# Which partition takes which token of an expert's block, in a one-core decoder step with a mixture of experts

## The chip, the cores and the metric

One core of a Trainium2 chip runs the whole program. The metric is the device time of one execution in microseconds (us), here 1616.77 us as the median of three runs. The core has a matrix engine (TensorE, PE), a vector engine (VectorE, DVE), a scalar engine (ScalarE, ACT), GpSimd (POOL) and SyncE (SP), and sixteen DMA engines that move data between device memory and the on-chip memory with its 128 partitions.

## What is computed

One layer of a hybrid decoder on 1024 prompt tokens and 32 sample tokens (1056 rows of 1024 float32 values): three token mixers, an output projection, and then a mixture of experts with 32 experts, of which each token uses two. The second half is where the change lies:

```python
def hier_moe(h, w_rg, b_rg, w_re, b_re, w1, w3, w2):
    ...
    g_sel = jnp.argmax(g_logits, axis=-1).astype(jnp.int32)
    e_in = e_logits[tok, g_sel]
    top_v, top_i = lax.top_k(e_in, TOP_K)
    ...
    def expert_block(args):
        xb, e = args
        return (jax.nn.silu(xb @ w1[e]) * (xb @ w3[e])) @ w2[e]
    ...
    return jnp.zeros((t, d), y_rows.dtype).at[tok_sorted].add(contrib)
```

An expert's weights are three matrices of 512 x 1024 float32, 6 MiB. The final normalisation of every row follows. Which rows of a block hold which of an expert's tokens makes no difference to the sum.

## The kernel before

The first 900 us or so are the dense part (mixers, projections), in items that PE takes one after the other. The routing then gives each (token, expert) pair a rank: the token's place among the tokens of its expert. `rank_ones` (L1262 to L1269) compares the ranks with the constant row `io128` and so makes a matrix of ones and zeros, token by slot; PE multiplies it with the tokens' numbers, and out comes `tok0`, a table of 128 partitions by 32 experts: partition p holds the token whose rank equals `io128[p]`. The same ones place each token's gate weight (`wslot`). Partitions whose number exceeds the ranks in use get an index out of bounds, and the indirect DMAs move nothing for them. With `io128` the row 0, 1, 2, ..., an expert with n tokens fills the partitions 0 to n-1.

The experts then run as 33 blocks b: one for each expert with up to 128 of its tokens, and the last one for the tokens beyond 128 of one expert. A block has 1056 x 2 / 33 = 64 tokens in the mean. For a block:

- SP loads six weight chunks `wr` of 1 MiB (L659), four for the up products, two for down. There are 13 slots; a load waits until PE has used the slot's last chunk. The slots that lie in the dense part's buffers get their first chunks as its last items free them (`moe_sync`).
- ACT rounds a chunk to `whr` (L1093), and DVE makes the remainder `wl` (L1281).
- POOL gathers the tokens' rows into `xg` (L786), one 4 KiB row for each filled partition; PE transposes them (step `T`, L893), and ACT and DVE split them into `xTh` and `xTl`.
- PE makes the up products (L902 to L904), DVE the gated hidden rows `gs`, PE transposes these (L910), DVE makes `gTl`, PE makes the down products `Y` (L919 to L921), and DVE multiplies by the gates: `ysb` (L1281).
- POOL adds `ysb` onto the rows of `x_rows` in device memory with an accumulating scatter (L790), again 4 KiB for each filled partition. `g2p` (L805) fetches gate rows where a slot changes kind.

PE's order is written out: in the turn of block b it does up(b,0), G(b-1), up(b,1), T(b+1), Y(b-1), up(b,2), up(b,3). The two last blocks are not scattered. Once block 30's scatter has landed, POOL fetches their rows of `x_rows` (L820), SP loads the tiles `yt`, ACT squares them and DVE scales and ends them (L1442), and POOL writes the late rows (L828).

The last block's table comes from a table in device memory whose rows go by rank itself, so that `io128` doesn't touch it.

Of the kernel before, what the change touches and what calls it, by code (L numbers as in the profile page):

```python
# [24 lines left out]
P = 128  # L25
# [56 lines left out]
def build(nc, x_prompt, x_sample, c_prompt, c_sample, state_conv_a, state_conv_c, norm1_g, norm2_g,  # L82
# [5 lines left out]
    with ctx:  # L88
        def sem(name):
            return ctx.enter_context(nc.semaphore(name))  # L90
# [12 lines left out]
        base = (nc.sbuf_base + 31) // 32 * 32  # L103
# [7 lines left out]
        def sb(name, shape, dt=F32):  # L111
            t, top[0] = at(name, shape, dt, top[0])
            return t
# [21 lines left out]
        io128 = sb("io128", [P, P])  # L135
# [426 lines left out]

        XT = [(g, t, rows) for g in range(2) for t, rows in tiles(g)]
        XN = {(g, t): n for n, (g, t, _) in enumerate(XT)}
        conv_flat = conv[:, :, :].rearrange("p c t -> p (c t)")

# [18 lines left out]
        rt_const, tab_out = sem("rt_const"), sem("tab_out")  # L585
# [1068 lines left out]
        def _(pool):  # L1654
            def x_load(g, t):
                s, rows = x_slot(g, t), dict(tiles(g))[t]
                if g and t == 0:
# [7 lines left out]
                               pattern=[[-1, P]], channel_multiplier=1).then_inc(id_ok, 1)  # L1665
# [27 lines left out]
            for p in range(KD // 2 - 1):  # L1693
                pool.wait_ge(modt_ok, p // 2 + 1)
                for k in (2 * p, 2 * p + 1):
# [9 lines left out]
                               pattern=[[0, HEADS], [-1, P]], channel_multiplier=1).then_inc(wsr_ok, 1)  # L1705
# [40 lines left out]
            for m, n in ((tri, P), (trif, NE)):  # L1746
                pool.affine_select(out=m[:], in_=m[:], compare_op=ALU.is_gt, fill=0.0, base=0,
                                   pattern=[[1, n]], channel_multiplier=-1).then_inc(rt_const, 1)
                pool.drain()
            pool.iota(io32[:], pattern=[[1, NE]], base=0, channel_multiplier=0,  # L1750
                      allow_small_or_imprecise_dtypes=True).then_inc(rt_const, 1)
            pool.drain()
            pool.iota(io16[:], pattern=[[1, MAXX]], base=0, channel_multiplier=0,
                      allow_small_or_imprecise_dtypes=True).then_inc(rt_const, 1)
            pool.drain()
            pool.iota(thr[:], pattern=[[P, NBLK - 1]], base=P, channel_multiplier=0,
                      allow_small_or_imprecise_dtypes=True).then_inc(rt_const, 1)
            pool.drain()
            pool.iota(bval[:], pattern=[[NE, NBLK - 1]], base=NE, channel_multiplier=1,
                      allow_small_or_imprecise_dtypes=True).then_inc(rt_const, 1)  # L1760
            pool.drain()
            pool.iota(io128[:], pattern=[[1, P]], base=0, channel_multiplier=0,
                      allow_small_or_imprecise_dtypes=True).then_inc(rt_const, 1)
            pool.drain()
            pool.iota(vhi[:], pattern=[[-(TPAD // P), 2], [-1, NT]], base=OOB // P, channel_multiplier=0,
                      allow_small_or_imprecise_dtypes=True).then_inc(rt_const, 1)
            pool.drain()
            pool.iota(vlo[:], pattern=[[0, 1]], base=OOB % P, channel_multiplier=-1,
                      allow_small_or_imprecise_dtypes=True).then_inc(rt_const, 1)
# [1508 lines left out]
```

## Time and profile before

| | us |
|---|---|
| median of three runs | 1616.77 (1615.28 to 1617.14) |
| the profiled execution | 1616.57 |
| its span, first to last instruction | 1614.8 |
| PE busy | 1555.9 |
| DVE busy | 1256.8 |
| ACT busy | 804.1 |
| POOL busy | 353.0 |

The profiled execution lies 0.20 us under the median. The page gives busy times by engine, the span in 40 slices of 40.4 us with the mean busy share of the sixteen DMA engines, the chain of work that ended last and the costliest groups. The blocks of the experts fill the slices from 25 on. A busy share is summed over packets, by the time each took; it isn't kept apart by DMA engine.

### The profile page before, as it was taken

What the parts mean: (1) busy time and instruction counts of PE and PEld (TensorE: products, weight loads), DVE (VectorE), ACT (ScalarE), POOL (GpSimd) and SP (SyncE); (2) the same over time, 40 slices, a digit from 0 to 9 for tenths busy, and PEclk for the clock granted to TensorE, in tenths of its full rate; (3) what the DMA queues carried; (4) which work ended last, traced back from release to release, by engine and by line L of the source; (5) the groups of instructions that cost most, each with busy time, mean ns of one, the idle gap of its engine ahead of it and who ended that gap; (6) DMA issues with size and microseconds to landing.
All of it is one profiled execution on the core that took longest, in us unless ns stands there. A gap on an engine that the chain in (4) does not pass through costs nothing.

```text
span 1614.8 us, 23286 instructions
## 1 busy us (share of the span) xinstructions
PE 1555.9 (96%) x9097; PEld 1333.5 (83%) x9097; DVE 1256.8 (78%) x1698; ACT 804.1 (50%) x878; POOL 353.0 (22%) x271
## 2 busy tenths in 40 slices
PE   5999999999999999999999998999999999999993
PEld 3777788878889999999999976888888888887771
DVE  4668877755838898887555568999999999899985
ACT  4222232334333323313243356887887787777773
POOL 2310000000000000002000202366655544333231
PEclk9999999999999999999999999999999999999997
DMA  9965223425434332224222866999999999999966
GB/s 339 321 198 181 80 86 90 139 79 147 130 91 144 118 88 77 78 88 140 78 79 84 275 225 241 359 391 387 384 368 376 380 387 379 382 371 368 372 242 236
DMA packets 219025, 362.48 MB, mean 224 GB/s; under 512 B 19807, under 2 KB 168383, under 8 KB 193562
## 3 DMA queue, kind: packets, MB, share of 16 engines
q1 hardware_dynamic: 196476, 323.10, 56.6%
q0 software_dynamic: 21792, 35.72, 7.6%
q10 hardware_dynamic: 646, 2.15, 0.3%
q8 instruction: 73, 1.20, 0.3%
q14 instruction: 38, 0.31, 0.1%
HBM read 363.16 MB, written 32.34 MB: 245 GB/s over the span
## 4 chain that ended last, share of the span: by engine, by line
PE 79%; DMA 10%; DVE 7%; issue 1%; DVEq 1%; ACT 1%; SPq 1%; POOLq 0%; POOL 0%; ACTq 0%
PE z L2930 16%; PE z L2932 16%; PE z L2931 16%; DMA wr<-in_w_dram 7%; PE z L904 5%; PE z L902 5%; PE z L903 5%; PE z L919 3%; PE z L921 3%; PE z L920 3%; DVE wl L1281 2%; PE q L2821 2%; DMA ada<-in_w_ada_dram 1%; PE q L893 1%; DVE conv L2350 1%
## 5 line engine op out<-in xcount | busy, mean ns | idle before, releaser
L1281 DVE TENSOR_TENSOR wl<-wr,whr 128x2048 fp32r<-128x2048 f32 x196 | 442.3, 2283 | 1.1 <-ACT whr L1093 0.8
L1093 ACT ACTIVATE whr<-wr 128x2048 fp32r<-128x2048 f32 x196 | 373.3, 1915 | 86.8 <-DMA wr<-in_w_dram 55.3
L2930 PE MATMUL z<-h_hi,w_hi 128*128 128x272 f32 (+1 forms) x1248 | 406.7, 326 | 2.3 <-DVE h_lo L2169 1.8
L2932 PE MATMUL z<-h_hi,w_lo 128*128 128x272 f32 (+1 forms) x1248 | 402.5, 323 | 0.0
L2931 PE MATMUL z<-h_lo,w_hi 128*128 128x272 f32 (+1 forms) x1248 | 401.3, 322 | 0.0
L2169 DVE TENSOR_TENSOR w_lo<-w_raw,w_hi 128x1024 fp32r<-128x1024 f32 (+1 forms) x168 | 179.4, 1068 | 127.3 <-ACT w_hi L1868 127.3
L2930 PEld LDWEIGHTS z<-h_hi,w_hi 128*128 128x128 f32 x1248 | 234.7, 188 | 28.2 <-issue 7.3
L2932 PEld LDWEIGHTS z<-h_hi,w_lo 128*128 128x128 f32 x1248 | 234.4, 188 | 16.6
L2931 PEld LDWEIGHTS z<-h_lo,w_hi 128*128 128x128 f32 x1248 | 234.8, 188 | 15.7 <-issue 0.2
L902 PE MATMUL z<-whr,xTh 128*128 128x512 f32 x528 | 208.8, 395 | 0.0
L904 PE MATMUL z<-wl,xTh 128*128 128x512 f32 x528 | 206.1, 390 | 0.0
L903 PE MATMUL z<-whr,xTl 128*128 128x512 f32 x528 | 205.5, 389 | 0.0
L2350 DVE SCALAR_TENSOR_TENSOR conv<-a_in,parT,conv 128x512 f32<-128x512 f32 x360 | 193.7, 582 | 14.5 <-issue 1.3
L1868 ACT ACTIVATE w_hi<-w_raw 128x1024 fp32r<-128x1024 f32 (+1 forms) x168 | 150.4, 929 | 45.6 <-DMA w_raw<-in_w_in_dram 45.3
L2046 ACT ACTIVATE sig<-z 128x512 f32<-128x512 f32 (+1 forms) x48 | 29.3, 610 | 266.1 <-PE z L2932 266.1
L805 POOL DMA_INDIRECT g2p<-mod_rows,g2i x33 | 78.6, 2383 | 257.5 <-ACT gfac L1081 239.8
L904 PEld LDWEIGHTS z<-wl,xTh 128*128 128x128 f32 x528 | 99.1, 188 | 21.1
L902 PEld LDWEIGHTS z<-whr,xTh 128*128 128x128 f32 x528 | 99.6, 189 | 19.5
L903 PEld LDWEIGHTS z<-whr,xTl 128*128 128x128 f32 x528 | 99.3, 188 | 19.6
L919 PE MATMUL z<-whr,gTh 128*128 128x512 f32 x256 | 102.8, 402 | 6.4 <-DVE gTl L1281 6.4
L921 PE MATMUL z<-wl,gTh 128*128 128x512 f32 x256 | 100.0, 391 | 0.0
L920 PE MATMUL z<-whr,gTl 128*128 128x512 f32 x256 | 99.9, 390 | 0.0
(480 smaller groups left out, 2291.5 us busy)
## 6 DMA issues: line engine op xcount, KB each, us to landing
wr<-in_w_dram SPq DMA_DIRECT2D x198, 1024.0 KB, 19.6
w_raw<-in_w_in_dram SPq DMA_DIRECT2D x104, 512.0 KB, 3.8
ada<-in_w_ada_dram SPq DMA_DIRECT2D x6, 2048.0 KB, 14.1
w_raw<-in_w_branch_dram SPq DMA_DIRECT2D x48, 256.0 KB, 2.8
w_raw<-in_w_out_dram SPq DMA_DIRECT2D x16, 512.0 KB, 3.9
ada_h<-in_w_ada_dram SPq DMA_DIRECT2D x2, 2048.0 KB, 15.3
ada_u<-in_w_ada_dram SPq DMA_DIRECT2D x2, 2048.0 KB, 9.9
ada_m<-in_w_ada_dram SPq DMA_DIRECT2D x2, 2048.0 KB, 10.7
```

What stands on the lines that cost most here:

```text
L902: pe.matmul(out, xTh[s][:, k, :], hi[:, i * FF:(i + 1) * FF], start=(k == 0), stop=False)
L903: pe.matmul(out, xTl[s][:, k, :], hi[:, i * FF:(i + 1) * FF], start=False, stop=False)
L904: last = pe.matmul(out, xTh[s][:, k, :], lo[:, i * FF:(i + 1) * FF], start=False, stop=(k == KD - 1))
L919: pe.matmul(out, gTh[:, k, :], hi[:, w0:w0 + 512], start=(k == 0), stop=False)
L1093: act.activation(whr[n % HN][:], wr[n % RN][:], ACT.Copy).then_inc(m_hi, 1)
L1281: return dve.tensor_tensor(out, a, b, op)
L1868: act.activation(w_hi[n % WS][:, 0:kn, :], w_raw[n % WS][:, 0:kn, :], ACT.Copy).then_inc(whi_ok, 1)
L2169: return dve.tensor_tensor(out, a, b, op)
L2350: last = dve.scalar_tensor_tensor(out, x, wt, out, ALU.mult, ALU.add)
L2930: pe.matmul(out, w_hi[w][:, k, :], hi[:, k, t0:t1], start=(k == 0), stop=False)
L2931: pe.matmul(out, w_hi[w][:, k, :], lo[:, k, t0:t1], start=False, stop=False)
L2932: last = pe.matmul(out, w_lo[w][:, k, :], hi[:, k, t0:t1], start=False, stop=(k == kn - 1))
```

## The change

One constant is made differently. The 128 values of the row `io128` are the same numbers in another order. Column 32j + 4a + b (j and b from 0 to 3, a from 0 to 7) holds 8(j//2) + 64(j%2) + a + 16b. Read the other way: an expert's tokens of rank 0 to 7 go to partitions 0, 4, 8, ..., 28, those of rank 8 to 15 to 64, 68, ..., 92, rank 16 to 23 to 1, 5, ..., 29, rank 24 to 31 to 65, 69, ..., 93, and so on; from rank 64 on the partitions 32 to 63 and 96 to 127 are filled in the same manner.

```diff
-            pool.iota(io128[:], pattern=[[1, P]], base=0, channel_multiplier=0,
-                      allow_small_or_imprecise_dtypes=True).then_inc(rt_const, 1)
+            for j in range(4):
+                i128 = pool.iota(io128[:, 32 * j:32 * j + 32], pattern=[[1, 8], [16, 4]], base=8 * (j // 2) + 64 * (j % 2),
+                                 channel_multiplier=0, allow_small_or_imprecise_dtypes=True)
+            i128.then_inc(rt_const, 1)
```

No other line differs. The loading of chunk slots as the last dense items free them stands in both kernels alike.

POOL's instructions around it, early in the program, in the kernel before; `io_58` is `io128`:

```order
L1756 IOTA thr 32x8
L1759 IOTA bval 32x8
L1762 IOTA io_58 128x128
L1765 IOTA vhi 128x18
L1768 IOTA vlo 128x1
L1771 IOTA vali 128x18
L1776 DMA wsS<-wsT 4x8x4 x8
```

The same place in the changed kernel, in which the lines after it are numbered two higher:

```order
L1759 IOTA bval 32x8
L1763 IOTA io_58 128x32 x4
L1767 IOTA vhi 128x18
L1770 IOTA vlo 128x1
L1773 IOTA vali 128x18
```

One instruction has become four; on the other engines nothing moves.

## Rows read from the trace of the kernel before

**Rows 1.** The page: span, PE, and DMA busy share in forty slices.
```profile
span 1614.8 us, 23286 instructions
...
PE 1555.9 (96%) x9097; PEld 1333.5 (83%) x9097; DVE 1256.8 (78%) x1698; ACT 804.1 (50%) x878; POOL 353.0 (22%) x271
...
DMA  9965223425434332224222866999999999999966
```

**Rows 2.** Chain that ended last, in time: start us, us, what.
```profile
1363.94 0.88 PE q L893 x8
1378.49 26.60 DMA wr<-in_w_dram
```

**Rows 3.** Timeline of PE: step T of blocks 20, 24, 32; Y behind the first.
```profile
1328.27 1.04 PE L893 MATMUL q<-ident,xg 128*128 128x128 f32 x8
1329.07 0.48 PE L919 MATMUL z<-whr,gTh 128*128 128x512 f32 x1
...
1399.29 1.04 PE L893 MATMUL q<-ident,xg 128*128 128x128 f32 x8
...
1548.38 1.04 PE L893 MATMUL q<-ident,xg 128*128 128x128 f32 x8
```

**Rows 4.** Chunks wr issued in 1026:1062, 1168:1204, 1310:1346, 1378:1454, in this order.
```profile
DMA to landing us min/median/max: 7.6/9.8/11.5
...
DMA to landing us min/median/max: 15.2/16.8/18.1
...
DMA to landing us min/median/max: 22.1/22.7/24.1
...
DMA to landing us min/median/max: 25.0/26.2/28.3
```

**Rows 5.** Windows: length, busy us of PE, PEld, DVE, ACT, POOL, PEclk, DMA share, GB/s.
```profile
1026.00:1399.00 373.00, 373.00 (x1767) 312.49 (x1766) 354.87 (x223) 298.77 (x208) 202.79 (x82) 1.00 1.01 382
1399.00:1548.00 149.00, 144.53 (x675) 119.72 (x675) 136.24 (x92) 115.23 (x81) 49.04 (x23) 1.00 1.01 373
```

**Rows 6.** DMA view of 1239:1275: GB/s in forty slices of 0.9 us.
```profile
GB/s 360 392 423 355 300 396 441 305 337 410 373 346 419 396 364 419 442 428 351 369 392 423 392 319 332 405 373 282 391 419 373 355 428 382 419 428 419 405 373 355
```

**Rows 7.** DMA view of 1026:1399: queue, packets, MB, share of 16 engines (q0: POOL).
```profile
q0 software_dynamic: 9604, 11.87, 12.5%
```

**Rows 8.** Waits in 1378:1454: who for whom, us, times, longest.
```profile
ACT whr L1093 <- DMA wr<-in_w_dram: 18.3, 26, 1.4
```

**Rows 9.** Timeline of PE at the end: Y(31), and the end of the up products.
```profile
1568.07 0.50 PE L919 MATMUL z<-whr,gTh 128*128 128x512 f32 x1 [1.00 <-DVE gTl L1281]
...
1579.09 1.02 PE L1033 MATMUL q<-ysb,same 128*128 128x512 f32 x2
```

**Rows 10.** Timeline of DVE: ysb of blocks 18 and 30, then the end.
```profile
1335.95 1.22 DVE L1281 TENSOR_TENSOR ysb<-z,gfac 128x1024 f32<-128x1024 f32 x1
...
1559.00 1.22 DVE L1281 TENSOR_TENSOR ysb<-z,gfac 128x1024 f32<-128x1024 f32 x1
...
1579.38 1.28 DVE L1442 SCALAR_TENSOR_TENSOR yt<-yt,fin,fgb 128x1024 f32<-128x1024 f32 x1
1580.59 0.68 DVE L1281 TENSOR_TENSOR gs<-hsg,z 128x512 f32<-128x512 f32 x1
1583.43 1.23 DVE L1281 TENSOR_TENSOR xg<-xg,ysb 128x1024 f32<-128x1024 f32 x1 [2.16 <-DMA xg<-x_rows,xtok]
```

**Rows 11.** Timeline of POOL: the scatters of blocks 18 and 30.
```profile
1337.97 2.88 POOL L790 DMA_INDIRECT x_rows<-ysb,tok  x1 [1.06 <-DVE ysb L1281]
...
1561.66 2.23 POOL L790 DMA_INDIRECT x_rows<-ysb,tok  x1 [1.67 <-issue]
```

**Rows 12.** Chain in time at the start of the experts: block 0's gather.
```profile
976.74 6.07 DMA xg<-h_rows,tok
```

**Rows 13.** Timeline of POOL: the iota, and its next wait.
```profile
85.31 0.25 POOL L1762 IOTA io<- 128x128 f32 x1
...
100.90 4.92 POOL L1776 DMA_DIRECT2D wsS<-wsT  x8 [14.43 <-ACTq L1919]
```

## The prediction

> **What bounds the kernel now.** I read the page's busy shares first, then the chain of work that ended last, and then the stretch of the experts in windows. PE is busy for 1555.9 of 1614.8 us, and the sixteen DMA engines show a 9 in 13 of the last 15 slices [rows 1]. Only that stretch uses the table that the change reorders. In it the chain changes hands: to 1364 us it goes by PE, one step T for each block, and from 1378 us on it comes back to weight chunks still in flight for 26.60 us [rows 2].
>
> The period of a block tells the same. From T(20) at 1328.27 to T(24) at 1399.29 it is 71.02 / 4 = 17.755 us, and PE has no gap in the 373 us to there. From T(24) to T(32) at 1548.38 it is 149.09 / 8 = 18.64 us [rows 3], with 4.47 us of gaps on PE [rows 5]. In the later part ACT waits for chunks 26 times in 76 us [rows 8]; PE's gaps follow from that through `whr` and `wl`.
>
> Why are chunks late only then? A chunk takes 9.8 us from issue to landing at the start, 16.8 eight blocks on, 22.7 after sixteen, and 26.2 where ACT waits [rows 4]. So behind PE's pace something falls back by (22.7 - 9.8) / 16 = 0.81 us in every block, until the 13 slots can't hide it. It isn't all sixteen DMA engines together: while the landing grows the core moves 382 GB/s in the mean [rows 5], and single slices of 0.9 us show 441 and 442 GB/s [rows 6], rates that no group of saturated engines would leave unused if all had a backlog. And a landing needs the last of the engines on which the chunk is spread. I conclude that some of them are behind while others idle. A share of 1.01 in both windows of rows 5 doesn't speak against it, since it is already 1.01 in the stretch in which PE never waits; packets of two queues that overlap on an engine are each counted in full.
>
> **What differs between engines.** Weight chunks fill all 128 partitions alike. The gathers and scatters of POOL move one row for each filled partition, and before the change these are the lowest 64 or so. POOL's queue takes 12.5% of the time of sixteen engines [rows 7]: 0.125 x 16 x 17.755 = 35.5 us of engine time a block. If one half of the engines carries nearly all of it, that is 4.4 us on each of eight; dealt out over sixteen it is 2.2. No trace shows which engine serves which partition.
>
> The Trainium skill (DMA: Bandwidth & Descriptors, "The descriptor swizzle") gives the map: partitions 0 to 63 go to engines 0 to 7, in fours, and 64 to 127 to engines 8 to 15. By it the new order gives sixteen consecutive ranks to sixteen different engines. It states this for whole transfers of 128 partitions; that it holds for indirect ones no row here shows.
>
> **The change part by part.** (1) Four iotas in place of one. One took 0.25 us; three more at up to 0.25 are 0.75 us on POOL, which next waits 14.43 us [rows 13]. Cost 0. Without that cover it would be 0.75 us on POOL's small stores alone.
>
> (2) The loaded engines' need per block. Now it is PE's period plus the drift, 17.755 + 0.81 = 18.56 us, near the 18.64 measured once the chunks set the pace. Less 2.2 us it is 16.4 us, 1.4 under PE's 17.755. The engines that were ahead need 18.6 - 4.4 = 14.2 now and also 16.4 then. So the drift should stop, and PE sets the period to the end. Saved to T(32): 149.09 - 8 x 17.755 = **7.1 us**. Bounds: 0 if the drift stays, 7.1 if it goes; I take 7.1, since 1.4 us a block is a wide margin. Blocks with 128 rows exceed it for a moment, which 13 slots hold.
>
> (3) From T(32) to the end of the up products. Y(31) starts 1568.07 - 1548.38 = 19.69 us after T(32) [rows 9]. At PE's own pace it is one period without the transposes of a next block: 17.755 + 0.80 (T to Y) - 0.88 (T itself) = 17.7 [rows 2, 3]. So 2.0 us are lost, of them 1.00 on `gTl`, which follows the transposed hidden rows in any case and which only T covers in other blocks. I take **1.0 us**, between 0 and 2.0.
>
> (4) `gs` of the last block. PE ends the up products at 1579.09 [rows 9], but DVE makes `gs` only at 1580.59, after ending a first tile `yt` at 1579.38 [rows 10]. That tile waits for block 30's scatter, so it goes with `ysb`(30). This comes 1559.00 - 1548.38 = 10.6 us after T(32), and for block 18 it came 1335.95 - 1328.27 = 7.7 us after T(20) [rows 3, 10]; and POOL issues 2.66 us after `ysb` starts, against 2.02 [rows 10, 11]. So the scatter moves 7.1 + 2.9 + 0.6 = 10.6 us ahead, and PE's up products only 7.1 + 1.0 = 8.1. The tile is then done at about 1570.0 and the up products at 1571.0, and the wait of 1.5 us goes but for the 0.3 between the two engines: **1.2 us**, bounds 0 and 1.5. What is late next: the fetch that DVE awaits at 1583.43 also moves by 10.6, to 1572.8; PE's last down products by 9.3. PE is the later again, and what DVE and POOL do after it is unchanged.
>
> (5) The first gather is on the chain for 6.07 us [rows 12]. It moves half as many rows on its busiest engines. At 35.5 us of engine time for two transfers of 64 rows a row takes at most 0.28 us, four rows fewer 1.1 us; part of that lies beside the fixed time. Bounds 0 and 1.1; I take **0.3**, since 6.07 us is far more than the engine time that the rows ask for (64 x 0.28 / 8 = 2.2).
>
> Sum: 7.1 + 1.0 + 1.2 + 0.3 = 9.6 us. Against the profiled execution 1616.57 - 9.6 = 1607.0; it stood 0.2 under the median, so 1607.2 us.
>
> **The rivals.** (a) One shared rate. If memory or fabric as a whole caps the loads near the 373 GB/s of the last stretch [rows 5], then spreading rows moves nothing: 1616.8 us. For it: share 1.01 throughout. Against it: 382 GB/s over 373 us and 442 in slices. The Trainium skill (DMA: Bandwidth & Descriptors, "Specifications") puts memory at about 358 GB/s for a core; by that all chunks would be late from the first block and the change worth nothing. The trace moves 382, so the measurement decides against it.
>
> (b) The change doesn't do what it says: POOL's transfers are dealt out by row and not by partition, the laggards are others, or every engine carries its fixed share already. 1616.8 us too. Against it: nothing else in the kernel treats partitions unequally.
>
> (c) Half a gain. A packet of a row costs the weights more than its own time by breaking their stream, and now does so on all sixteen. If the need falls only to 18.2 us a block, the drift is 0.45 in place of 0.81; the 16 us of cushion that were used up by T(24) then last nearly to T(32). Most of the 7.1 is won, some of the tail isn't: 1609 to 1612.
>
> (d) Slower. If the busy shares are exclusive time, sixteen even engines need 1.01 x 18.64 = 18.83 us a block, and with interleaving on all of them perhaps 19.0. The drift is then 1.25 us, the cushion of 16 us is gone after 13 of the 29 blocks behind T(3), and the other 16 lose 1.25 us each: 20 us against 7.1 now, 1629.7 us. It decides from a need of 18.56 us on, which is that of today's slow half. Against it: a share of 1.01 is seen where PE never waits.
>
> (e) More: steps 3 to 5 at their upper bounds give 7.1 + 2.0 + 1.5 + 1.1 = 11.7: 1605.
>
> **How the numbers follow.** The forecast has 0.70, (e) 0.05, (c) 0.10, (a) and (b) together 0.11, (d) 0.04. The range 1604.5 to 1612.0 holds the first three, 0.85. A change under 0.2%, 3.2 us, can't be told from none. Faster by more: 0.70 + 0.05 + 0.10 = 0.85; same 0.11; slower 0.04.
>
> **What would show it.** Step 2: the median time to landing of `wr` stays near 10 us up to the last block, and T follows T at 17.75 us to T(32), with ACT's waits for `wr` in 1378:1454 gone from 18.3 to under 5. If the landing grows at the same pace, (a) or (b) holds; at half the pace, (c). Step 3: Y(31) 18 to 19 us after T(32). Step 4: `gs` right after PE's last up product, and `ysb`(30) 7.7 us after T(32). Step 5: the first gather under 6.07 us. I am wrong if the queue of POOL keeps some engines behind whatever partitions it fills.

## The result, and the profile after

The changed kernel takes 1603.56 us (median of four; 1603.14 us at the least) against 1616.8: a ratio of 0.9919, with a 95% interval from 0.9900 to 0.9938. One of the four took 1737.90 us at a lower granted clock (0.849 for 0.992 to 0.994) and is left out of the ratio; the median of the other three is 1603.39. A second comparison on another occasion gave 0.9917 (0.9900 to 0.9933). That is 13.2 us, where 9.6 were forecast, and 0.9 us under the lower end of the range.

The page of the changed kernel: span, the engines' busy shares, the chain that ended last by engine, and the median landing of a weight chunk (after the count and the KB).

```profile
span 1601.6 us, 23289 instructions
...
PE 1553.2 (97%) x9097; PEld 1332.6 (83%) x9097; DVE 1256.5 (78%) x1698; ACT 802.3 (50%) x878; POOL 375.2 (23%) x274
...
PE 90%; DVE 6%; DMA 1%; DVEq 1%; issue 1%; ACT 1%; POOLq 0%; POOL 0%; SPq 0%
...
wr<-in_w_dram SPq DMA_DIRECT2D x198, 1024.0 KB, 7.6
```

PE's own work has hardly changed (2.7 us less busy), but DMA is gone from the chain: 1%, and the four stays on chunks in flight, of the kind in [rows 2] and 25.9 to 28.1 us long, aren't there.

Weight chunks of the changed kernel, issue to landing, for the four stretches of [rows 4]:

```profile
DMA to landing us min/median/max: 7.4/7.9/9.6
...
DMA to landing us min/median/max: 6.4/7.1/8.4
...
DMA to landing us min/median/max: 6.2/7.1/8.0
...
DMA to landing us min/median/max: 6.2/7.4/8.5
```

No drift is left: 7 to 8 us in all four (8.9 in a stretch between, 1097:1133), where it grew from 9.8 to 26.2. The two windows of the changed kernel that answer to [rows 5] (length, busy us by engine, PEclk, DMA share, GB/s):

```profile
1026.00:1399.00 373.00, 373.00 (x1767) 312.48 (x1766) 355.62 (x224) 300.49 (x211) 207.63 (x82) 1.00 1.01 387
1399.00:1545.00 146.00, 146.00 (x693) 122.38 (x691) 139.57 (x94) 118.41 (x84) 62.14 (x23) 1.00 1.01 386
```

PE now has no gap in the second either, and the core moves 386 GB/s there for 373. The DMA share is 1.01 in all four windows, with the drift and without. The steps T(24) and T(32), as in [rows 3]:

```profile
1397.76 1.04 PE L893 MATMUL q<-ident,xg 128*128 128x128 f32 x8
...
1540.01 1.04 PE L893 MATMUL q<-ident,xg 128*128 128x128 f32 x8
```

Y(31) and the end of the up products, as in [rows 9]:

```profile
1557.75 0.50 PE L919 MATMUL z<-whr,gTh 128*128 128x512 f32 x1
...
1568.75 1.02 PE L1033 MATMUL q<-ysb,same 128*128 128x512 f32 x2
```

The gain by stretches, from the two traces (spans 1614.8 and 1601.6, difference 13.2):

| stretch | before | after | gain | forecast |
|---|---|---|---|---|
| start to T(24) | 1399.29 | 1397.76 | 1.5 | 0.3 |
| T(24) to T(32) | 149.09 | 142.25 | 6.8 | 7.1 |
| T(32) to the end | 66.4 | 61.6 | 4.8 | 2.2 |

The end of the changed kernel on DVE, which answers to [rows 10] (start, us, operation, and in brackets the idle time before with what ended it):

```profile
1547.69 1.22 DVE L1281 TENSOR_TENSOR ysb<-z,gfac 128x1024 f32<-128x1024 f32 x1
...
1568.95 0.69 DVE L1281 TENSOR_TENSOR gs<-hsg,z 128x512 f32<-128x512 f32 x1 [2.00 <-PE z L904]
1570.13 1.23 DVE L1281 TENSOR_TENSOR xg<-xg,ysb 128x1024 f32<-128x1024 f32 x1 [0.49 <-DMA xg<-x_rows,xtok]
...
1574.87 0.69 DVE L1281 TENSOR_TENSOR ysb<-z,gfac 128x512 f32<-128x512 f32 x1 [0.30 <-PE z L1047]
```

and the last of these steps in the kernel before:

```profile
1588.04 0.69 DVE L1281 TENSOR_TENSOR ysb<-z,gfac 128x512 f32<-128x512 f32 x1 [0.17 <-issue]
```

From this half of the last `ysb` on both kernels need the same 26.8 us to the end (1614.8 - 1588.04, 1601.6 - 1574.87). So the end is decided by what releases it. After: PE, after a short wait. Before: DVE came to it straight from its own work, which had begun late, at 1583.43, when the fetch of the late rows landed [rows 10]. That is 4.6 us from landing to `ysb`, all but 0.2 of it DVE's work.

### The profile page after: what moved, and what is told of

Same layout as the page of the kernel before. It is cut to its first block, busy times and chain, and to the rows that moved or that the text cites. A ratio compares the mean times of both kernels' runs of the same rounds, so it can differ in the third digit from the quotient of the medians.

```text
span 1601.6 us, 23289 instructions
## 1 busy us (share of the span) xinstructions
PE 1553.2 (97%) x9097; PEld 1332.6 (83%) x9097; DVE 1256.5 (78%) x1698; ACT 802.3 (50%) x878; POOL 375.2 (23%) x274
## 4 chain that ended last, share of the span: by engine, by line
PE 90%; DVE 6%; DMA 1%; DVEq 1%; issue 1%; ACT 1%; POOLq 0%; POOL 0%; SPq 0%
PE z L2932 16%; PE z L2934 16%; PE z L2933 16%; PE z L904 7%; PE z L902 7%; PE z L903 7%; PE z L919 4%; PE z L921 4%; PE z L920 4%; PE q L893 2%; PE q L2823 2%; PE q L2842 1%; DVE conv L2352 1%; DMA ada_h<-in_w_ada_dram 1%; DVE wl L1281 1%; PE q L910 1%
## 5 line engine op out<-in xcount | busy, mean ns | idle before, releaser
L805 POOL DMA_INDIRECT g2p<-mod_rows,g2i x33 | 91.1, 2760 | 226.5 <-ACT gfac L1081 210.9
```

## The experiments

The kernels differ from the kernel before in the lines shown, unless said otherwise; where only added lines are shown, they stand in place of the iota of `io128`, or of the old form of the same line. Times are compared with runs of the kernel before on the same chip.

### The same eight engines in another order

```diff
+            for j in range(4):
+                i128 = pool.iota(io128[:, 32 * j:32 * j + 32], pattern=[[1, 8], [8, 4]], base=32 * j,
+                                 channel_multiplier=0, allow_small_or_imprecise_dtypes=True)
+            i128.then_inc(rt_const, 1)
```

> The kernel before, but the tokens of a block are dealt out with a stride of four over partitions 0 to 63 (rank 0 to 7 to partitions 0, 4, ..., 28, rank 8 to 15 to 1, 5, ..., 29, and so on; rank 32 to 63 in the same way to 32 to 63, and only ranks from 64 on to the upper half). By the map of partitions to engines in the Trainium skill (DMA: Bandwidth & Descriptors, The descriptor swizzle) these are the same eight engines as before, only in another order. Theory A (what counts is how many DMA engines share the rows): the landing time of a weight chunk grows as before, T(32) comes as late as before up to 1 us, time 1614 to 1617.5 us. Theory B (what counted was that neighbouring partitions were used together, or that the order of the rows changed at all): landing stays at 7 to 8 us and the time is that of the changed kernel, 1603 to 1605 us.

Measured: 1608.72 us, ratio 0.9952 (0.9936 to 0.9969): neither theory. Chunks in 1026:1062, 1310:1346 and 1454:1527:

```profile
DMA to landing us min/median/max: 7.0/9.3/12.1
...
DMA to landing us min/median/max: 15.6/16.5/17.1
...
DMA to landing us min/median/max: 21.7/24.1/26.5
```

The drift is there, but slower, and the 13 slots just hide it: T(24) to T(32) takes 142.43 us, all but 0.2 us the full pace, as its rows show.

```profile
1398.96 1.04 PE L893 MATMUL q<-ident,xg 128*128 128x128 f32 x8
...
1541.39 1.04 PE L893 MATMUL q<-ident,xg 128*128 128x128 f32 x8
```

What the expectation overlooked is that the eight aren't even among themselves. By the routing of the reference's inputs, computed from the reference, the 32 experts' blocks have between 24 and 128 tokens; with slots from 0 upward a block of 36 or more already fills all eight partitions of the first group (0 to 3 and 32 to 35), while the last one (28 to 31 and 60 to 63) gets its fifth row only with the 61st token. Dealing over 0 to 63 evens this out. So it isn't neighbourhood, and not only how many engines share the rows: what counts is how many rows lie on the busiest one.

### The other half

```diff
+            pool.iota(io128[:], pattern=[[-1, P]], base=P - 1, channel_multiplier=0,
+                      allow_small_or_imprecise_dtypes=True).then_inc(rt_const, 1)
```

> The kernel before with each slot on partition 127 - rank: the rows fill the upper half from the top. Theory A (any half of the engines is as bad as any other): as the kernel before, 1615 to 1618 us, landing of a chunk up to 26 us. Theory C (the engines of the lower half are slower by themselves, or carry other work of the kernel besides the rows): the drift is clearly smaller on the upper half, T(32) at least 3 us earlier, 1604 to 1612 us.

Measured: 1616.25 us, ratio 0.9998 (0.9989 to 1.0008), with the chunks of 1378:1454 at

```profile
DMA to landing us min/median/max: 25.1/26.2/28.5
```

the 26.2 us of [rows 4]. Theory A. The lower half has no handicap of its own.

### Nine engines

```diff
+            for h in range(2):
+                for jj in range(2):
+                    c = 64 * h + 32 * jj
+                    n = 5 - h
+                    pool.iota(io128[:, c:c + 4 * n], pattern=[[1, n], [9, 4]], base=5 * h + 36 * jj,
+                              channel_multiplier=0, allow_small_or_imprecise_dtypes=True)
+                    i128 = pool.iota(io128[:, c + 4 * n:c + 32], pattern=[[1, 8 - n], [7, 4]], base=72 + 3 * h + 28 * jj,
+                                     channel_multiplier=0, allow_small_or_imprecise_dtypes=True)
+            i128.then_inc(rt_const, 1)
```

> The kernel before with the first 72 ranks dealt round-robin over nine groups of eight partitions (five in the lower half, four in the upper), which by the Trainium skill (DMA: Bandwidth & Descriptors, The descriptor swizzle) are nine engines, and the other 56 ranks over the rest. POOL's 35.5 us of engine time a block then lie on nine: 3.9 us each in place of 4.4, so the need falls from 18.56 to 18.1 us and the drift from 0.81 to about 0.3 us a block. Theory A: landing rises from 8 to 13 to 18 us over the 29 blocks, which the 13 slots hide, so that T(32) comes at the full pace (T(24) to T(32) 142 us) although the drift goes on; the end gains only in part: 1603.5 to 1607 us. Theory D (every engine counts alike, the gain grows with the number of engines in proportion): 1616.8 - 13.2 / 8 = 1615 us.

Measured: 1605.09 us, ratio 0.9928 (0.9912 to 0.9945). Chunks in 1454:1527:

```profile
DMA to landing us min/median/max: 16.6/18.6/21.2
```

T(24) and T(32):

```profile
1398.77 1.04 PE L893 MATMUL q<-ident,xg 128*128 128x128 f32 x8
...
1541.02 1.04 PE L893 MATMUL q<-ident,xg 128*128 128x128 f32 x8
```

142.25 us: the full pace over a drift that goes on, as theory A has it. One engine more than in `same_eight` takes 3.6 us off the time. In the two traces it is 3.2 us, and 2.8 of them lie behind T(32): 65.7 us to the end there, 62.9 here (spans 1607.1 and 1603.9).

### Quarters swapped, without fine dealing

```diff
+            for j in range(4):
+                i128 = pool.iota(io128[:, 32 * j:32 * j + 32], pattern=[[1, 32]], base=32 * (0, 2, 1, 3)[j],
+                                 channel_multiplier=0, allow_small_or_imprecise_dtypes=True)
+            i128.then_inc(rt_const, 1)
```

> The kernel before with the two middle quarters of the partitions swapped: ranks 0 to 31 on partitions 0 to 31, 32 to 63 on 64 to 95, 64 to 95 on 32 to 63. No fine dealing: a block of 32 tokens still uses only the lower half. Theory A: an engine gets eight rows a block only where a block has over 64 tokens, so that in the mean it stays under PE's period; time within 1.5 us of the changed kernel, 1603 to 1605 us. Theory E (the fine dealing by sixteen is what matters): clearly between the two, 1607 to 1613 us.

Measured: 1603.32 us, ratio 0.9918 (0.9902 to 0.9935), the time of the changed kernel. Chunks in 1168:1204 and 1454:1527:

```profile
DMA to landing us min/median/max: 11.6/12.2/13.0
...
DMA to landing us min/median/max: 7.2/9.3/10.8
```

Theory A. The fullest stretch is blocks 4 to 8, with 128, 127, 69, 91 and 73 tokens. Over it and a little beyond the landing goes up, and then it comes down again, which the slots hide. So the gain needs only that the busiest engine stays under PE's period in the mean.

The four maps and the change can be put in one row. The Trainium skill (DMA: Bandwidth & Descriptors, "The descriptor swizzle") says which partitions an engine serves; with the token counts of the blocks 2 to 31 that gives the mean rows a block on the busiest engine. Beside it stands the median landing in 1454:1527:

| kernel | rows on the busiest | landing us | time us |
|---|---|---|---|
| before | 7.5 | 25.9 | 1616.8 |
| same_eight | 6.9 | 24.1 | 1608.7 |
| nine_engines | 6.6 | 18.6 | 1605.1 |
| quarters | 5.7 | 9.3 | 1603.3 |
| the change | 4.5 | 7.9 | 1603.6 |

The traces agree with the page's map, for POOL's indirect transfers too: the landings fall in the order of the rows, and the mirrored map is as slow as the kernel before. The amount fits as well. The prediction's 35.5 us a block for 2 x 64 rows make 0.55 us for a row that is gathered and scattered; this is an estimate, and a high one, since it counts all that POOL's queue moves. By it `same_eight` with 0.66 rows less needs 0.36 us less a block, and `nine_engines` with 0.96 rows less 0.53 us. Between 1026:1062 and 1310:1346 the drift went from 0.81 us a block to (16.5 - 9.3) / 16 = 0.45 in `same_eight` and to 0.34 in `nine_engines` (8.0 to 13.5 us). No row names an engine, though: anything else that the same groups of partitions share would give the same order.

### No rows in the scatters

```diff
-                                        bounds_check=TOK - 1, oob_is_err=False, compute_op=ALU.add).then_inc(done, 16)
+                                        bounds_check=0, oob_is_err=False, compute_op=ALU.add).then_inc(done, 16)
```

> The kernel before, in which the accumulating scatters move no row but that of token 0, so that the experts' outputs of blocks 0 to 30 are not added; gathers, loads and order are the same, and the slots lie as before. Theory A (the rows on one half of the engines cause the drift): the drift goes away without any change of the slots; landing of a chunk stays under 12 us, T(24) to T(32) is 142 us, time 1602 to 1605 us. Theory F (it isn't the rows, but which partitions hold tokens, for instance their effect on PE, ACT or DVE): 1615 to 1618 us.

Measured: 1604.75 us, ratio 0.9924 (0.9908 to 0.9941). With the slots of the kernel before, chunks in 1310:1346:

```profile
DMA to landing us min/median/max: 6.8/7.2/8.2
```

where it was 22.7. Theory A: the rows are the load. Taking away the scatters' half of them is enough to end the drift. This run takes away load and leaves the slots, so by itself it doesn't speak for the map.

### Light scatters from block 22 on

```diff
+            def scatter_dma(s, col, done, rows=TOK):
...
+                                        bounds_check=rows - 1, oob_is_err=False, compute_op=ALU.add).then_inc(done, 16)
...
+                scatter_dma(b % 2, tok0[:, b:b + 1] if b < NE else xtok[:, 0:1], m_sc[b % 2], 1 if b >= 22 else TOK)
```

> The kernel before, slots as before, in which the scatters of blocks 22 to 30 move only token 0's row, so that these blocks' outputs are not added; the blocks to 21 are as before. Theory A (the drift and the end both hang on the backlog of chunks at the time): landing of a chunk grows to 22 us as before until block 22 and then falls under 12; T(24) to T(32) takes 142 us; the last fetch no longer holds DVE up, so that from T(32) to the end it is 61.6 us and not 66.4; time 1616.6 - 7.1 - 4.8 = 1604.7, within 1 us. Theory B (the end is late for another reason than the backlog and block 30's rows): T(24) to T(32) 142 us, but 65 us or more from T(32) to the end, 1608 to 1610 us.

Measured: 1606.16 us, ratio 0.9933 (0.9916 to 0.9949), over the expected point by 1.5 us. Chunks in 1378:1454 and 1454:1527, and T(24) and T(32):

```profile
DMA to landing us min/median/max: 19.1/22.0/25.2
...
DMA to landing us min/median/max: 12.9/15.1/17.6
```

```profile
1399.43 1.04 PE L893 MATMUL q<-ident,xg 128*128 128x128 f32 x8
...
1542.81 1.04 PE L893 MATMUL q<-ident,xg 128*128 128x128 f32 x8
```

The landing was to fall under 12 us and was still at 15.1 in the last stretch. T(24) to T(32) took 143.4 us and not 142: the backlog went down more slowly than I thought, and two periods were still long. From T(32) to the end (span 1604.5) it is 61.7 us. That is theory A's number, the changed kernel's own, with the slots as before: the 4.8 us of the end hang on the backlog and block 30's rows. Which of the two has more of it this run doesn't part.

### A later scatter in the changed kernel

In the changed kernel:

```diff
+                if b == NB - 3:
+                    pool.wait_ge(m_c, up_no(NB - 1, 0) + 1)
```

> The changed kernel, in which POOL holds back the scatter of block 30 until PE has used the first up chunk of block 32, some 4.2 us later than now (about 1554.5 for 1550.3 us). Theory G (in the changed kernel the way over this scatter, the fetch of the late rows and DVE lies only 0.3 us under PE's, so that before it was this way that set the end): the fetch lands 4 us later and the time rises by 3.5 to 4.2 us, to 1607.0 to 1607.8 us. Theory H (PE's last down products set the end in both, with room over the scatter's way): the time rises by less than 1 us, under 1604.6 us.

Measured: 1607.93 us beside 1603.54 for the changed kernel: 4.4 us more, 0.2 over what theory G allowed. The scatter itself came 5.9 us later (1556.24 for 1550.34), not 4.2; POOL, DVE and PE there, and a window in which PEclk is the third number from the end:

```profile
1556.24 2.35 POOL L790 DMA_INDIRECT x_rows<-ysb,tok  x1 [7.54 <-issue]
```

```profile
1571.68 0.68 DVE L1283 TENSOR_TENSOR gs<-hsg,z 128x512 f32<-128x512 f32 x1
1574.37 1.23 DVE L1283 TENSOR_TENSOR xg<-xg,ysb 128x1024 f32<-128x1024 f32 x1 [2.02 <-DMA xg<-x_rows,xtok]
1579.08 0.69 DVE L1283 TENSOR_TENSOR ysb<-z,gfac 128x512 f32<-128x512 f32 x1 [0.27 <-PE z L1049]
```

```profile
1572.42 1.13 PE L912 MATMUL q<-ident,gs 128*128 128x128 f32 x4 [2.62 <-DVE gs L1283]
...
1573.00:1575.00 2.00, 2.00 (x5) 0.97 (x4) 0.63 (x1) 1.42 (x2) 0.00 (x0) 0.50 1.01 391
```

The fetch is awaited to 1574.37 (1570.13 without the delay), and the half `ysb` moves by the same 4.2 us. But what released this `ysb` was PE. The late scatter also holds up the tile `yt` that goes before `gs`, so `gs` came 2.7 us later, PE waited 2.62 us for it, and what followed ran at a granted clock of 0.50 (1.00 in the changed kernel's trace). DVE's own way, 1574.37 + 4.6, ends at 1579.0, 0.1 us before. So theory H is refuted, and both ways hang on this scatter; that the way over the fetch alone would have moved the end is not shown by this run. How near the two lie in the changed kernel is read from its own rows: 1570.13 + 4.6 = 1574.7 on DVE, and PE's release at 1574.87.

The changed kernel as it is, run beside these:

> The changed kernel beside the kernel before on this chip, for the comparison with the two others of this call: 1603 to 1604 us, ratio 0.991 to 0.993.

Measured: 1603.54 us, 0.9917 (0.9900 to 0.9933).

### The clock at the first transposes

The first step T of the kernel before and of the changed kernel, and the window 983:986 of each (PEclk is the third number from the end):

```profile
983.06 1.94 PE L893 MATMUL q<-ident,xg 128*128 128x128 f32 x8 [3.06 <-DMA xg<-h_rows,tok]
...
983.00:986.00 3.00, 2.94 (x23) 2.91 (x24) 0.00 (x0) 0.96 (x1) 0.23 (x1) 0.52 0.71 232
```

```profile
982.34 1.13 PE L893 MATMUL q<-ident,xg 128*128 128x128 f32 x8 [1.79 <-DMA xg<-h_rows,tok]
...
983.00:986.00 3.00, 2.58 (x32) 2.22 (x31) 1.43 (x2) 1.02 (x1) 1.60 (x2) 1.00 0.90 284
```

After 3.06 us of idling the granted clock was 0.52, about the lower of the two levels (1.2 GHz of 2.4), and T took 1.94 us; after 1.79 us it was 1.00 and T took 1.13. The length of the wait alone doesn't decide it. `same_eight` waited 2.31 us and fell to 0.52, while `nine_engines` with 2.46 us and `no_scatter_rows` with 2.83 us kept 1.00.

```diff
-            keep_busy(pe, 21)
+            keep_busy(pe, 32)
```

> The kernel before with 32 in place of 21 small matmuls ahead of the first step T, so that PE idles under 1 us and not 3.06 us while block 0's gather is under way. In the kernel before, T(0) ran at a granted clock of 0.52 and T(1) came 9.91 us after it, in the changed kernel at 1.00 and 9.08 us. Theory A (0.8 us of the changed kernel's gain hang on the clock at T(0), which the longer gather let fall): T(0) at clock 1.00, T(1) 9.1 us after it, everything behind 0.8 us earlier, 1615.0 to 1616.5 us. Theory B (the slots' order itself makes the first block quicker): T(1) stays 9.9 us behind T(0).

Measured: 1617.95 us, ratio 1.0007 (0.9998 to 1.0017). T(0) and T(1):

```profile
982.95 1.13 PE L893 MATMUL q<-ident,xg 128*128 128x128 f32 x8 [0.28 <-DMA xg<-h_rows,tok]
992.03 1.05 PE L893 MATMUL q<-ident,xg 128*128 128x128 f32 x8
...
1548.72 1.04 PE L893 MATMUL q<-ident,xg 128*128 128x128 f32 x8
```

Theory A is right on the mechanism (T(1) follows at 9.08 us) and wrong on the time: T(32) comes no earlier than in [rows 3]. The 0.9 us gained at T(1) (992.03 for 992.97) were lost before any chunk was late. PE waits some 2 us ahead of G(0) in both kernels; in this run the granted clock then fell, in the kernel before it did not. The wait, the window behind it and T(2) here:

```profile
1003.26 0.82 PE L910 MATMUL q<-ident,gs 128*128 128x128 f32 x4 [1.98 <-issue]
...
1003.00:1006.00 3.00, 2.74 (x9) 2.31 (x10) 3.00 (x3) 1.88 (x2) 2.67 (x1) 0.62 0.82 333
...
1008.17 1.05 PE L893 MATMUL q<-ident,xg 128*128 128x128 f32 x8
```

and in the kernel before:

```profile
1003.00:1006.00 3.00, 1.81 (x10) 1.62 (x11) 2.92 (x5) 1.06 (x2) 1.75 (x1) 1.00 1.00 393
...
1007.51 1.04 PE L893 MATMUL q<-ident,xg 128*128 128x128 f32 x8
```

T(24) came 0.2 us earlier than in the kernel before (1399.08), and the late chunks took that too. So this run can't say what the saving is worth at the end. The changed kernel kept it: T(2) came 1.5 us earlier than before (1005.99 for 1007.51), as T(1) and T(24) did.

## Why the prediction was wrong

The direction, the mechanism and the largest term were right. What failed is the time from T(32) to the end: the sum had it 2.2 us shorter and it got 4.8 us shorter, of which 1.5 us lay behind `gs`, where the prediction had put nothing.

**Reading of the bound: right.** The drift of the landing marked one part of the DMA engines as late while the mean share and rate said nothing. `mirror`, `same_eight`, `nine_engines` and `no_scatter_rows` show it from four sides, and ACT's 18.3 us of waits for `wr` [rows 8] are gone after the change.

**Step 1: right.** The three more iotas are hidden.

**Step 2: right, 6.8 us for 7.1.** The forecast period of 17.755 us held but for one block, in which an extra product has its place; 142.25 us for eight periods instead of 142.0. The inner reasoning was coarser than it looked: "4.4 us on each of eight" took the eight as even. `same_eight` moved them by less than a row (7.5 to 6.9 on the busiest) and had 6.7 of the 6.8 us between T(24) and T(32).

**Steps 3 and 4: the term that failed, 4.8 us for 2.2.** The step said of the time behind `gs`: "PE is the later again, and what DVE and POOL do after it is unchanged". I measured how far PE's last products move and took that for the end. The 4.8 us have three parts, all from rows shown above:

| | before | after | gain | forecast |
|---|---|---|---|---|
| T(32) to the end of the up products | 30.71 | 28.74 | 2.0 | 1.0 |
| from there to `gs` | 1.50 | 0.20 | 1.3 | 1.2 |
| `gs` to the last half `ysb` | 7.45 | 5.92 | 1.5 | 0 |

The last line is the path that the prediction had wrong. In the kernel before PE was not the later of the two: at the 5.92 us that PE needs from `gs` the half `ysb` could have come at 1586.5, and it came at 1588.04, behind the fetch of 1583.43 and DVE's own 4.6 us. The "again" took PE as the later before the change too, and gave no time to DVE's work behind the fetch. In the first line a size was off: of the 2.0 us lost to Y(31) I kept 1.0 as a dependence on `gTl` that only T covers, and in the changed kernel Y(31) starts 17.7 us after T(32) with no such wait. The second line was right.

**Step 5: too small, 1.5 us for 0.3.** The chain's row for the first gather after the change:

```profile
977.29 4.81 DMA xg<-h_rows,tok
```

4.81 us for the 6.07 of [rows 12]: 1.3 us, above the upper bound of 1.1. The gathers of the other runs bear it out. Block 0 has 54 tokens, which by the map are 8 rows on the busiest engine before and 4 after. From the end of POOL's instruction to the landing (6.07 - 2.33 = 3.7 us in the kernel before) the traces' chains have 3.4 to 3.6 us in the four other runs with 8 rows, 3.0 in `same_eight` with 7 and in `nine_engines` with 6, and 2.4 to 2.5 in all four runs with 4. So four rows are 1.0 to 1.3 us, nearly the whole of the bound, and that the rows lie beside the fixed time was wrong. The granted clock was a gain that the prediction didn't have: T(0) to T(1) is 9.09 us now, 0.8 less. It is partly luck: of the runs with a gather as long as before and the same small matmuls, `mirror` and `light_from_22` lost the 0.8 us too (9.96 and 9.92 us from T(0) to T(1)), but `no_scatter_rows` did not (9.12), after 2.83 us of waiting. Of these 2.1 us the trace shows 1.5 at T(24), because the dense part of this run reached the gather 0.55 us later.

**The rivals.** (a) and (b), nothing changes, are refuted by the time and by `no_scatter_rows`; 386 GB/s are moved at PE's full pace, over the about 358 GB/s of the Trainium skill (DMA: Bandwidth & Descriptors, "Specifications"), which the prediction had already set aside. (c), half a drift, did not happen in the change, but `nine_engines` is that case and shows what it is worth: the stretch in full, the end in part. (d) is refuted by the landings. (e), all small terms at their upper bounds, came nearest with 1605, and was given 0.05. The lower end of the range was drawn at that case, though it left out a term, the end behind `gs`, which had been set to nothing without a bound. Its 11.7 us and these 1.5 make the 13.2 measured; that the sum fits so well is in part chance, since step 5 was 0.4 us over its bound and steps 2 and 4 together 0.5 under theirs.

## What to carry to other kernels

A mean busy share of the DMA engines can't tell an even load from a lopsided one. Read the time from issue to landing of equal transfers over the run. Here it grew from 9.8 to 26.2 us while single slices still moved 442 GB/s, and the cause was that the rows of the gathers and scatters lay mostly on one half of the partitions. For an end that several ways reach, take each way with all the work behind it up to the step where they meet, and compare them there.

## What the runs showed of the hardware

- Which partitions a gather or scatter uses was worth 13.2 us with the same bytes, packets and, but for three iotas, instructions. Swapping two quarters of the partitions was enough (1603.32 us).
- The DMA share was 1.01 with a landing that grows to 26 us and with one that stays at 7 to 9 us.
- The landings follow the rows on the busiest engine, by the map: 25.9, 24.1, 18.6, 9.3 and 7.9 us in the last stretch for 7.5, 6.9, 6.6, 5.7 and 4.5 rows a block.
- The first gather took 3.4 to 3.7 us behind POOL's instruction with 8 rows on the busiest engine and 2.4 to 2.5 us with 4.
- A gather that lasted 1.3 us longer let PE idle 3.06 us instead of 1.79, and the following transposes ran at a granted clock of 0.52. Waits of 2.46 and 2.83 us in other runs left it at 1.00, and one of 1.98 us in `more_busy` was followed by 0.62.
